# Low half of the split weights: an adding DMA in place of a GpSimd subtraction

## What is computed

```python
for i in range(DEPTH):                      # two layers
    xp = half_swiglu(xp, norm_w[i, 0], w_ffn_in[i, 0], w_ffn_out[i, 0])
    if i % N_MIXERS == 0: yp = ssd_mixer(rms_norm(xp, norm_w[i, 1]), ...)      # Mamba-2 SSD
    else:                 yp = dilated_mixer(rms_norm(xp, norm_w[i, 1]), ...)  # windowed attention
    xp = half_swiglu(xp + yp, norm_w[i, 2], w_ffn_in[i, 1], w_ffn_out[i, 1])
# half_swiglu: x + 0.5 * (silu(a) * b) @ w_out with a, b = split(rms_norm(x, g) @ w_in)
```

## Time and profile before

| | us |
|---|---|
| median of 3 runs | 2869.78 (2869.76 to 2872.54) |
| span of the profiled execution (the only time shown of it) | 2876.5 |
| PE busy | 2763.0 (96%) |
| PEld busy | 2676.7 (93%) |
| VectorE busy | 1377.6 (48%) |
| GpSimd busy | 1009.6 (35%) |
| ScalarE busy | 756.6 (26%) |
| loads of raw weights | 345, of 512 and 704 KB |

### The profile page before, as it was taken

One profiled execution on the slowest core, in us unless ns is written; L12 is line 12 of the kernel. 1 busy time (PEld: TensorE's weight loads), 2 busy tenths in 40 slices (PEclk: granted clock), 3 DMA queues, 4 the chain that ended last, 5 costly groups with the idle time before them and its releaser, 6 DMA issues.

```text
span 2876.5 us, 50563 instructions
## 1 busy us (share of the span) xinstructions
PE 2763.0 (96%) x20359; PEld 2676.7 (93%) x20359; DVE 1377.6 (48%) x2151; ACT 756.6 (26%) x1001; POOL 1009.6 (35%) x516
## 2 busy tenths in 40 slices
PE   8999998999999979999999999999999998999997
PEld 8999998888888868999999999999889887999997
DVE  6344118888888877344213444212343445544302
ACT  3222223333333333222222222222222223222211
POOL 3344333444443432344333443333122210433432
PEclk9999998999999988999999999999999997999999
DMA  3222222222222212222222222224232320222221
GB/s 117 87 80 83 88 78 85 84 85 71 79 74 90 90 54 82 87 80 80 89 86 74 80 80 84 87 77 166 99 107 100 105 78 15 81 82 86 85 86 67
DMA packets 65342, 243.64 MB, mean 85 GB/s; under 512 B 9281, under 2 KB 10945, under 8 KB 62081
## 3 DMA queue, kind: packets, MB, share of 16 engines
q1 hardware_dynamic: 65280, 242.78, 26.1%
HBM read 223.44 MB, written 19.32 MB: 84 GB/s over the span
## 4 chain that ended last, share of the span: by engine, by line
PE 86%; DVE 10%; issue 3%; ACT 1%; DVEq 0%; DMA 0%; SPq 0%; ACTq 0%
PE ps L820 24%; PE ps L826 24%; PE ps L821 24%; DVE sb_acc L1337 2%; PE ps L1104 1%; PE ps L1047 1%; PE ps L945 1%; PE ps L1127 1%; PE ps L984 1%; PE ps L1091 1%; PE ps L1073 1%; PE ps L958 1%; PE ps L986 1%; PE ps L985 1%; PE ps L934 1%
## 5 line engine op out<-in xcount | busy, mean ns | idle before, releaser
L438 POOL TENSOR_TENSOR sb_wl<-sb_raw,sb_wh 128x1024 fp32r<-128x1024 f32 (+1 forms) x345 | 915.2, 2653 | 1749.9 <-ACT sb_wh L543 1749.9
L820 PE MATMUL ps<-sb_uh,sb_wh 128*128 128x288 f32 (+1 forms) x4176 | 1140.6, 301 | 18.9 <-ACT sb_wh L543 14.8
L821 PE MATMUL ps<-sb_ul,sb_wh 128*128 128x288 f32 (+1 forms) x4176 | 1133.2, 297 | 0.0
L820 PEld LDWEIGHTS ps<-sb_uh,sb_wh 128*128 128x128 f32 x4176 | 796.4, 191 | 26.7 <-ACT sb_wh L543 11.4
L821 PEld LDWEIGHTS ps<-sb_ul,sb_wh 128*128 128x128 f32 x4176 | 794.9, 190 | 0.8
L543 ACT CAST sb_wh<-sb_raw 128x1024 fp32r<-128x1024 f32 (+1 forms) x345 | 382.0, 1107 | 1256.4 <-PE ps L826 1170.5
L826 PE MATMUL ps<-sb_uh,sb_wl 128*128 128x288 f32 (+1 forms) x4176 | 597.5, 296 | 0.0
L826 PEld LDWEIGHTS ps<-sb_uh,sb_wl 128*128 128x128 f32 x4176 | 570.4, 189 | 0.0
L821 PE MATMUL ps<-sb_hl,sb_wh 128*128 128x288 f32 x1408 | 376.4, 296 | 0.0
L820 PE MATMUL ps<-sb_hh,sb_wh 128*128 128x288 f32 x1408 | 376.4, 296 | 0.0
L1243 DVE TENSOR_TENSOR sb_up<-ps,sb_rms 128x576 f32<-128x576 f32 x88 | 66.6, 757 | 445.6 <-PE ps L826 445.6
(11 more groups left out here) (223 smaller groups left out, 2466.5 us busy)
## 6 DMA issues: line engine op xcount, KB each, us to landing
sb_raw<-w_ffn_in SPq DMA_DIRECT2D x176, 512.0 KB, 3.6
sb_raw<-w_ffn_out SPq DMA_DIRECT2D x64, 704.0 KB, 4.1
sb_raw<-w_ssd SPq DMA_DIRECT2D x64, 512.0 KB, 3.7
sb_raw<-w_att SPq DMA_DIRECT2D x40, 512.0 KB, 3.7
sb_h<-state SPq DMA_DIRECT2D x8, 1024.0 KB, 6.0
ssm_sample<-sb_h SPq DMA_DIRECT2D x8, 1024.0 KB, 4.8
sb_kc<-k_cache SPq DMA_DIRECT2D x16, 512.0 KB, 4.4
sb_vc<-v_cache SPq DMA_DIRECT2D x8, 1024.0 KB, 5.9
```

Of the source, the lines that this page charges most:

```text
L438: pool.tensor_tensor(wl[:, parity, 0:width], raw[:, parity, 0:width], wh[:, parity, 0:width].bitcast(F32), ALU.subtract).then_inc(wl_done, 1)
L820: pe.matmul(ps[:, b, 0:n], w, rh[:, k, t0:t0 + n], start=first and k == 0, stop=False)
L821: pe.matmul(ps[:, b, 0:n], w, rl[:, k, t0:t0 + n], start=False, stop=False)
```

## The change

ScalarE gets a second instruction for each unit: behind the rounding it writes the negated, rounded weights into `wl`. GpSimd no longer subtracts; it issues a DMA that adds `raw` onto `wl` where it lies, so that `wl` becomes raw - rounded. The DMA signals one of two semaphores, by the parity of the unit (`wl_in`), and counts 16 for each landing; PE's low half, PE's two output projections and SyncE's next load into the same `raw` buffer wait for it. GpSimd's loops are written out, turn by turn; the other engines keep theirs, and the functions get the loop index, the units per turn and the unit apart (`i, per, u`), from which `landed` works out the count to wait for.

```diff
-        wh_done, wl_done, unit_done = sem("wh_done"), sem("wl_done"), sem("unit_done")
+        wh_done, nh_done, unit_done = sem("wh_done"), sem("nh_done"), sem("unit_done")
+        wl_in = [sem("wl_in0"), sem("wl_in1")]
...
+        def landed(i, per, u):
+            return i * (8 * per) + 16 * (u // 2 + 1)
...
-            def unit(u, parity, src, width):
-                if not (isinstance(u, int) and u < 2):
-                    sp.wait_ge(wl_done, u - 1)
-                sp.dma_start(raw[:, parity, 0:width], src).then_inc(raw_in[parity], 16)
+            def unit(i, per, u, src, width):
+                if not isinstance(i, int) or u + per * i >= 2:
+                    sp.wait_ge(wl_in[u % 2], landed(i, per, u - 2))
+                sp.dma_start(raw[:, u % 2, 0:width], src).then_inc(raw_in[u % 2], 16)
...
-            def low_part(u, parity, width):
-                pool.wait_ge(wh_done, u + 1)
-                pool.tensor_tensor(wl[:, parity, 0:width], raw[:, parity, 0:width],
-                                   wh[:, parity, 0:width].bitcast(F32), ALU.subtract).then_inc(wl_done, 1)
+            def low_part(i, per, u, width):
+                pool.wait_ge(nh_done, i * per + (u + 1))
+                pool.dma_start(wl[:, u % 2, 0:width], raw[:, u % 2, 0:width],
+                               accum_op=ALU.add).then_inc(wl_in[u % 2], 16)
...
-                with pool.Fori(0, KF // 2) as i:
+                for i in range(0, KF // 2):
...
                 nc.scalar.copy(wh[:, u % 2, 0:width], raw[:, u % 2, 0:width]).then_inc(wh_done, 1)
+                nc.scalar.activation(wl[:, u % 2, 0:width], raw[:, u % 2, 0:width], ACT.Copy, scale=-1.0).then_inc(nh_done, 1)
...
-                pe.wait_ge(wl_done, u + 1)
+                pe.wait_ge(wl_in[parity], landed(i, per, u))
```

More of the change, by code:

```diff
@@ L413, in attention @@
                 u = U_FFN[3] - 1
-                unit(u, u % 2, io["w_att"][PAIRS - 1, 9], UW)
+                unit(0, 10, u, io["w_att"][PAIRS - 1, 9], UW)
                 store_k(PAIRS - 1)
@@ L502, in group @@
                     else:
-                        low_part(U_FFN1 - 1, (U_FFN1 - 1) % 2, UW)
+                        low_part(0, 8, U_FFN1 - 1, UW)
                 conv_state(0)
                 for k in range(5):
[L507 to L510, removed]
+                    low_part(0, 8, U_GRP + k, UW)
+                new_conv_state(0, lambda: low_part(0, 8, U_GRP + 5, UW))
+                low_part(0, 8, U_GRP + 6, UW)
+                for g in range(0, GROUPS - 1):
                     group(g, False)
@@ L521, in attention @@
                         pool.memset(qa[:, :, :].rearrange("p g r -> p (g r)"), 0.0).then_inc(qa_zero, 1)
-                with pool.Fori(0, PAIRS - 1) as c:
+                for c in range(0, PAIRS - 1):
                     for k in range(10):
                         u = U_ATT + 9 + k
-                        low_part(c * 10 + u, u % 2, UW)
-                low_part(U_FFN[3] - 1, (U_FFN[3] - 1) % 2, UW)
+                        low_part(c, 10, u, UW)
+                low_part(0, 10, U_FFN[3] - 1, UW)
             ffn(0)
@@ L811, in _, with product @@
         def _(pe):
-            def product(u, parity, nk, rh, rl, banks, split, first=True, last=True, chunk=None):
-                pe.wait_ge(wh_done, u + 1)
+            def product(i, per, u, nk, rh, rl, banks, split, first=True, last=True, chunk=None):
+                parity = u % 2
+                pe.wait_ge(wh_done, i * per + (u + 1))
                 for k in range(nk):
@@ L1162, in turn @@
                         ahead(8)
-                    u = U_FFN[3] - 1 if last else c * 10 + (U_ATT + 18)
-                    parity = (U_ATT + 18) % 2 if not last else u % 2
-                    pe.wait_ge(wh_done, u + 1)
-                    pe.wait_ge(wl_done, u + 1)
+                    i, u = (0, U_FFN[3] - 1) if last else (c, U_ATT + 18)
+                    parity = u % 2
+                    pe.wait_ge(wh_done, i * 10 + (u + 1))
+                    pe.wait_ge(wl_in[parity], landed(i, 10, u))
                     pe.wait_ge(ol_done, c + 1)
```

69 lines of the change are left out of this document (34 added, 35 removed).

## The result

The changed kernel takes 2978.35 us in the median of four runs, beside 2871.16 us for four runs of the kernel before: ratio 1.0357, 95% interval 1.0321 to 1.0393. It is slower, by 3.6%; the forecast was 2.6%, on the 2869.78 us known then. The profiled execution has a span of 2965.2 us and 2967.19 us of time, the lowest of its four runs; it stands 89 us over the profiled execution before, while the medians are 107 us apart.

A forecast was written before the change was run, and what follows sets the result against it. PE was taken to bound the kernel (86% of the chain), sharing it with VectorE in SSD. Feed-forward-in 75.6, SSD -13 and attention 12.5 gave +75 us on 2869.8: 2945 us, 2.6% slower, range 2842 to 3290.

The forecast's parts named there:

- The value of X: Time from the negation's end to the adding DMA's landing, GpSimd's issue included; forecast 7.7 us, bounded by 5.3 and 10.8.
- raw-buffer bound: Feed-forward-in: the next raw load stalls once X exceeds 6.8 us; each us beyond lengthens PE's unit by 0.5.
- Company: 1.7 us added to the add's 6.0 us because it overlaps the other buffer's load.
- the first rival's case: Quick add, X = 5.3 us: feed-forward loses 0, SSD gains 31 us, attention loses 5; 2844 us, faster; chance 29%.
- Feed-forward-in +75.6 us: Loss in 4 stages of 44 units, less the first two of each: 168 x (7.7 - 6.8)/2.
- my formula: Feed-forward-in: each unit beyond a stage's first two loses (X - 6.8)/2 us, in all four stages.
- Feed-forward-out 0: The 1408-wide units lose nothing, as X of 7.7 us is under 9.3.
- the bound of 9.3 for X: Feed-forward-out: the low half is in time for PE's read while X is under 9.3 us.
- Attention +12.5 us: PE waits for the output unit's low half, landing at 2235.2 against a read from 2231.05: +4.2 us x 3 turns.
- SSD -13 us: Per turn, -3.1 us from VectorE freed of GpSimd's subtraction, +1.2 from the late output low half: -1.9 x 7 turns.
- The estimate of 4.4 us: The add's time by the Trainium skill's figures; by them the add would be hidden, as with X = 5.3.
- The queues and the fetches, 0: Stores and loads queued behind a waiting raw load, GpSimd's own products, and its unrolled loops' instruction fetches cost 0.

The follow-up runs named there:

- e2: Changed kernel with the adding DMA covering only the first half of each unit's columns, part of the computation left out: 2860.07 us, ratio 0.9903.
- e5: Changed kernel with negation before rounding, SyncE's loops written out and its load also waiting for the rounded copy: 2887.30 us, ratio 1.0001.
- e7: Changed kernel with the GpSimd DMA copying raw weights instead of adding, subtraction left out: 2861.24 us, ratio 0.9919.
- e9: Changed kernel with feed-forward-in raw loads halved from each block's fifth unit on, so values are wrong: 2898.01 us, ratio 1.0053.
- e12: Changed kernel with DMA add only for every second feed-forward unit, GpSimd subtraction for all others: 2884.70 us, ratio 1.0020.
- e10: Changed kernel, rounding still first, with SyncE's loops written out and the raw load also waiting for the rounded copy: 2946.69 us, ratio 1.0227.
- e1: Changed kernel with the add onto the negated copy done by a GpSimd instruction instead of a DMA: 2895.82 us, ratio 1.0034.
- e8: Changed kernel with DMA add only for the SSD turns' projection units, GpSimd subtraction elsewhere: 2868.97 us, ratio 0.9948.
- e3: Changed kernel with DMA add only in the feed-forward blocks, GpSimd subtraction in SSD and attention: median 2973.27 us, four runs over 80 us.
- e11: Changed kernel with DMA add only for SSD projection units, negation before rounding for those, SyncE's loops written out: 2866.29 us, ratio 0.9970.
- e4: Changed kernel with DMA add only in SSD and attention, GpSimd subtraction in feed-forward: 2902.58 us, ratio 1.0057.
- e13: The changed kernel run again unaltered, for its spread and a second profile: 2970.87 us, ratio 1.0330.

## Why the prediction was right

The mechanism that I priced highest, the closed wait for the raw buffer, is the one that costs most, and by about what I said. That the total came out near is in part luck: one term (SSD) was off by 29 us with the wrong sign, another (attention) was met by waits other than the one it was made of, and the measured 107 us stand beside a forecast of 75.

**The value of X and the raw-buffer bound** (right, with two terms off that cancel, which is luck). X is 1719.92 to 1727.20, 7.3 us, where I had 7.7; the load beside it takes 4.2 to 4.3 us, which I had left at 3.6. Their sum, which is what the lap sees, is 11.5 us against my 11.3, and the units take 6.9 us as forecast.

**Company** (right as a cause, wrong as a constant). I gave each add 1.7 us for it. Alone the add takes 4.5 us, so X is 4.8 us, which would have been the first rival's case; started together with a load it takes 7.0. Both are in one trace. The kernel is slow because the lap that the collision makes (13.7 us) is longer than PE's 12.8, and the collision keeps the lap long. Each edit that takes enough off the lap (e2, e5, e7, e9) makes it fall apart, and so does e12, which keeps add and load from meeting. e10, at 13.4 us, is still over and keeps its collision.

**Feed-forward-in +75.6 us**: measured +66. By my formula all four blocks lose; three did (18.5, 21.0 and 23.0 us, 0.5 us a unit), and the second, in its staggered pattern, lost 3.4. **Feed-forward-out 0**: right, the adds of 704 KB take 6.1 us, far from the bound of 9.3 for X.

**Attention +12.5 us**: +12 in the two traces, but not for my reason. I had PE wait 4.2 us for the low half of the output unit, three times. The changed kernel in one turn (casts, the add's issue, PE's first matmul of the output), and below it PE's longest wait in the stage:

```profile
2286.58 1.05 ACT L549 CAST sb_wh<-sb_raw 128x1024 fp32r<-128x1024 f32 x1
...
2288.89 0.86 POOL L444 DMA_DIRECT2D sb_wl<-sb_raw  x1 [7.72 <-ACT sb_wl L550]
...
2293.49 0.36 PE L1181 MATMUL ps<-sb_oh,sb_wh 128*128 128x256 f32 x1 [1.03 <-issue]
```

```profile
PE ps L1067 <- issue: 5.6, 2, 2.8
```

The add takes 4.5 us here, the time of one alone, and lands at 2293.4, so X is 4.8 us and not 7.7. By my own formula that makes 2227.5 + 4.8 - 2231.05 = 1.25 us a turn; from cast to output PE took 6.9 us where it had taken 5.7, and it stood still for 1.0 us each time, 3 us in all. PE stood still for 8.7 us more in the stage than before (23.4 against 14.7), and 5.6 of them are the two waits at line 1067. "Issue" means that the profile shows nothing that PE waited for. These waits are in every kernel but before and e1, also where attention has no DMA add (5.4 us in e8), so the adds do not make them; what does is open. As means over traces the difference is 15 us (468 to 486 us with GpSimd's subtraction or add in before, e1, e3, e8, e11, e12; 488 to 496 us with the full DMA add in e4, e5, e9, e10, e13 and the changed kernel), and the same work wanders by some 9 us around its mean.

**SSD -13 us**: this is the step that failed. SSD took 680 to 690 us in the five traces with the whole DMA add and the rounding first (mean 684.5: changed, e4, e9, e10, e13), 674 in the mean of before, e3 and e12, and 659 in e8 and e11. So:
- The gain was real, (674 - 659)/7 = 2.2 us a turn where I had 3.1, with six of the eight subtractions of a turn gone. Line 1344 takes 837/844/846 ns as min/median/max, where one had taken 2926.
- The loss was (684.5 - 659)/7 = 3.6 us a turn, not 1.2: the two output units, which e8 and e11 leave to GpSimd.
- A part of such a loss needs no DMA: e1, where GpSimd adds and the low half is only later by the negation, has SSD at 689 us, (689 - 674)/7 = 2.1 us a turn over the kernels with the subtraction.

The chain of waits of the changed kernel in one turn shows the loss (start us, us, what):

```profile
653.46 0.35 SPq L346
654.06 6.74 DMA sb_raw<-w_ssd
661.20 0.65 issue
661.85 1.06 ACT sb_wl L550
662.91 0.28 issue
663.19 6.59 DMA sb_wl<-sb_raw
669.83 0.58 PE ps L992
670.41 0.21 PE ps L993
...
676.31 0.15 PE ps L992
...
679.14 1.12 PE ps L894 x4
```

The raw load of the second output unit takes 6.7 us, where it took 5.5 before (5.6 us with the signals). It is issued behind the state store of line 346 (653.46), as before, and now also overlaps the last 1.8 us of the first output unit's add; which of its neighbours slows it is not shown. That is the first term I left out: I moved the add but kept the load's old landing. With it the wait is 5.2 us, where my numbers made it 802.55 - 799.39 = 3.2. The second is larger. For the work from the low half's landing to the next turn I counted 6.4 us. The rows before have 8.42 us from 799.39 to 807.81; the 6.4 leaves out a wait for VectorE, which they do not show and which stands in the timeline before:

```profile
804.36 0.39 PE L984 MATMUL ps<-sb_gh,sb_wh 128*128 128x256 f32 x1 [1.54 <-DVE sb_x L1499]
```

In the changed kernel 669.8 to 679.14 are 9.3 us, with no such wait. PE had stood still for 5.2 us, and then its clock was down. Stretches of the changed kernel, before and after 676 us:

```profile
670.00:676.00 6.00, 6.00 (x26) 6.00 (x27) 0.83 (x3) 0.29 (x2) 1.20 (x5) 0.51 0.81 172
676.00:679.00 3.00, 3.00 (x24) 2.87 (x22) 1.63 (x4) 0.00 (x0) 0.00 (x0) 1.00 0.39 98
```

0.51 is the level of 1.2 GHz, half of 2.4: 26 matmuls in 6 us, then 24 in 3 us. So in this turn a wait of 5.2 us cost about 3 us more. At the same place of the other turns the granted clock reads 0.51 or 0.52 in four (from 590, 747.5, 986.4 and 1065) and 0.76 over 7 us in two (from 829.4 and 907.9), where the loss is about half of that. My sentence "the granted clock stays near 1.00" held for feed-forward and failed here: over 500 to 1030 us it is 0.96, with 0.99 before and 1.00 in e8. The output projection's matmuls, which are in SSD alone, show it without a timeline (busy us, mean ns of one); page rows of the changed kernel, e5, e8 and e2:

```profile
L992 PE MATMUL ps<-sb_gh,sb_wh 128*128 128x256 f32 (+1 forms) x256 | 84.6, 331 | 43.5 <-DMA sb_wl<-sb_raw 34.9
```

```profile
L993 PE MATMUL ps<-sb_gh,sb_wh 128*128 128x256 f32 (+1 forms) x256 | 82.0, 320 | 32.6 <-DMA sb_wl<-sb_raw 23.5
```

```profile
L1017 PE MATMUL ps<-sb_gh,sb_wh 128*128 128x256 f32 (+1 forms) x256 | 78.9, 308 | 23.7 <-DVE sb_zs L1379 14.1
```

```profile
L992 PE MATMUL ps<-sb_gh,sb_wh 128*128 128x256 f32 (+1 forms) x256 | 79.2, 309 | 24.1 <-DMA sb_wl<-sb_raw 15.0
```

The mean of one goes 331, 320, 308, 309 ns as SSD goes 688, 672, 659, 649 us. It is 325 ns in e1, where PE waited there for VectorE. How long a wait is enough for this I can't say. In e1 and in e8 PE stood still for the same 2.0 us ahead of a block of the projection; these are the 4 us behind the wait, in e1 and then in e8:

```profile
724.80:728.80 4.00, 4.00 (x18) 4.00 (x19) 2.26 (x6) 3.43 (x5) 1.55 (x1) 0.57 0.94 317
```

```profile
710.70:714.70 4.00, 4.00 (x30) 4.00 (x31) 3.21 (x6) 2.49 (x4) 2.42 (x1) 1.00 0.88 317
```

The clock fell in the one (0.57) and not in the other (1.00).

**The estimate of 4.4 us.** From the Trainium skill ("DMA: Bandwidth & Descriptors", section Anatomy of one DMA, with "Collectives: The Full Stack", section The bandwidth ceiling) came an estimate of 4.4 us for the add. The trace agrees for an add alone, 4.5 us; for one that starts with a load, 7.0 us, it does not.

**The queues and the fetches, 0**: right for GpSimd. For SyncE's loop code I had no term, and with the added wait it turned out to be worth 29 us in e10's feed-forward-in, through the lap.

What stays open: why a load that starts in the first 2 us of an add slows both, while one that starts 1.7 us earlier and is still in flight slows neither (e9: 4.5 and 2.6 us; e5: 4.6 and 3.5 us). The runs show the order of issue and the times, not where in the engines they meet. Open too are what puts a block into one pattern or the other, and the 18 us between the profiled executions and the medians.

## What to carry to other kernels

When a copy is moved from an engine to a DMA, close the loop of its buffer (load, cast, add, load) and sum it with the durations that they have in each other's company: if the lap is under the consumer's time for the same units the DMA is free, and if it is just over, each us of it costs every unit half a us, and small things in it (the order of two copies, a loop's code) decide whether the loss stays: 66 us at a lap of 13.7 us here, 37 at 13.4, none once a copy was off it. Give the DMA those units whose result is needed late (here the SSD projections, 0.3 to 0.5% faster than before), and leave to the engine those that PE waits for. A wait of PE of some us is to be priced at more than its length where the trace shows the clock at half after it. And check each term of a forecast that came true by its own rows: the attention stage met its 12 us without the wait that was forecast for it.

## What the runs showed of the hardware

- An adding DMA of 512 KB within SBUF, issued by GpSimd, landed after 4.5 us alone, 256 KB after 3.3 us (e2); a plain copy of 512 KB after 2.9 us (e7). Its issue held GpSimd for 0.86 us, the copy's for 0.53 us.
- Issued 0.1 to 0.3 us ahead of a 512 KB load from HBM it mostly took 6.7 to 7.1 us and the load 4.2 to 4.4 instead of 3.5; 0.9 to 1.1 us ahead of it 5.5 to 5.8 us and the load 5.6 to 6.3; with the load 1.5 us or more ahead, mostly 4.5 to 4.9 us.
- A coupled pair of buffers held two steady patterns in one execution, 6.9 us a unit and about 9.0/3.8 us in pairs (6.4 a unit), for over thirty units each.
- After a wait of PE of 5.2 us the granted clock was 0.51 for some 6 us. After one of 2.0 us it was 0.57 over 4 us in e1 and 1.00 in e8.
